# The opening of a one-core transformer step: rows for silu loaded first, weights of two groups behind them without waits, norm weights spread by a matmul, x issued behind silu

## What is computed

```
mod = silu(c) @ w_mod + b_mod                      # c_ctx for the context tokens
shift1, scale1, gate1, shift2, scale2, gate2 = split(mod, 6)
h   = layer_norm_plain(x) * (1 + scale1) + shift1
z   = h @ w_in                                      # q, k, v, xr, gr
q, k = rms_norm(q, q_norm_g), rms_norm(k, k_norm_g) # then rotary on latent tokens
mix = concat(attention(q, k, v), rg_lru(xr, gr)) @ w_out
x   = layer_norm(ALPHA * x + gate1 * mix)
x   = layer_norm(ALPHA * x + gate2 * expert_choice_ffn(h2))   # 16 experts
```

## Time and profile before

| | us |
|---|---|
| median of 3 runs | 945.56 (943.97 to 945.8) |
| profiled execution | 944.97 |
| its span | 943.2 |
| TensorE (PE) busy in the span | 882.9 |
| VectorE (DVE) busy | 774.0 |
| ScalarE (ACT) busy | 576.1 |
| GpSimd (POOL) busy | 160.8 |
| first matmul of group 0 | 12.88 |
| first transpose of x | 39.02 |

### The profile page before, as it was taken

One profiled execution on the slowest core, in us unless ns is written; L12 is line 12 of the kernel. 1 busy time (PEld: TensorE's weight loads), 2 busy tenths in 40 slices (PEclk: granted clock), 3 DMA queues, 4 the chain that ended last, 5 costly groups with the idle time before them and its releaser, 6 DMA issues.

```text
span 943.2 us, 11657 instructions
## 1 busy us (share of the span) xinstructions
PE 882.9 (94%) x4643; PEld 602.8 (64%) x4643; DVE 774.0 (82%) x802; ACT 576.1 (61%) x588; POOL 160.8 (17%) x108
## 2 busy tenths in 40 slices
PE   2899999889999976999999999999999999999995
PEld 0389978356678843666666666666666666666663
DVE  2777736578779887888989989998998998998877
ACT  1344367735751343777777777777777777677653
POOL 1000300010011014203203303303302311320220
PEclk9899999999999986999999999999999999999999
DMA  8930500663048387999999999999999999999716
GB/s 281 396 129 1 207 1 1 262 162 114 1 152 314 138 322 286 362 419 386 415 393 385 417 389 392 410 396 391 401 403 387 390 409 382 384 414 388 275 15 200
DMA packets 57358, 272.81 MB, mean 289 GB/s; under 512 B 6788, under 2 KB 7032, under 8 KB 40920
## 3 DMA queue, kind: packets, MB, share of 16 engines
q1 hardware_dynamic: 48264, 242.76, 65.7%
q0 software_dynamic: 7600, 24.06, 9.2%
q10 hardware_dynamic: 1440, 5.24, 1.4%
HBM read 258.05 MB, written 14.00 MB: 288 GB/s over the span
## 4 chain that ended last, share of the span: by engine, by line
PE 85%; DMA 5%; DVE 5%; ACT 2%; issue 1%; SPq 1%; ACTq 0%; DVEq 0%
PE PS L918 24%; PE PS L920 24%; PE PS L919 24%; DMA ring<-in_w_mod 4%; PE PS L932 2%; PE PS L1081 2%; PE PS L1065 2%; PE PS L1035 1%; PE PS L1104 1%; PE PS L1223 1%; PE PS L1236 1%; DMA acc_scratch<-ysc,idx_u 1%; PE PS L1159 1%; DVE smin L1558 1%; ACT prob L721 1%
## 5 line engine op out<-in xcount | busy, mean ns | idle before, releaser
L1737 DVE TENSOR_TENSOR Wl<-wr,Wh 128x2048 fp32r<-128x2048 f32 x190 | 432.4, 2289 | 50.1 <-ACT Wh L832 50.1
L832 ACT ACTIVATE Wh<-wr 128x2048 fp32r<-128x2048 f32 x192 | 367.3, 1915 | 67.6 <-PE PS L920 67.6
L918 PE MATMUL PS<-Wh,Xh 128*80 128x512 f32 x512 | 202.4, 395 | 1.5 <-DVE Xl L1742 0.8
L920 PE MATMUL PS<-Wl,Xh 128*80 128x512 f32 x512 | 201.0, 393 | 0.0
L919 PE MATMUL PS<-Wh,Xl 128*80 128x512 f32 x512 | 200.8, 392 | 0.0
L543 POOL DMA_INDIRECT acc_scratch<-ysc,idx_u x15 | 81.2, 5410 | 418.6 <-DVE ysc L1768 418.6
L920 PEld LDWEIGHTS PS<-Wl,Xh 128*80 128x80 f32 x512 | 75.7, 148 | 42.1
L918 PEld LDWEIGHTS PS<-Wh,Xh 128*80 128x80 f32 x512 | 75.7, 148 | 41.8 <-issue 1.2
L918 PE MATMUL PS<-Wh,HTh 128*80 128x512 f32 x256 | 101.6, 397 | 0.0
L919 PEld LDWEIGHTS PS<-Wh,Xl 128*80 128x80 f32 x512 | 75.8, 148 | 39.4
L919 PE MATMUL PS<-Wh,HTl 128*80 128x512 f32 x256 | 100.4, 392 | 0.0
(11 more groups left out here) (298 smaller groups left out, 1211.4 us busy)
## 6 DMA issues: line engine op xcount, KB each, us to landing
wr<-in_w_gate_up SPq DMA_DIRECT2D x128, 1024.0 KB, 13.6
wr<-in_w_down SPq DMA_DIRECT2D x64, 1024.0 KB, 12.3
ring<-in_w_mod SPq DMA_DIRECT2D x24, 1024.0 KB, 9.0
xt<-in_x_sample ACTq DMA_DIRECT2D x8, 512.0 KB, 8.6
ring<-in_w_in SPq DMA_DIRECT2D x4, 1024.0 KB, 12.4
ring<-in_w_out SPq DMA_DIRECT2D x4, 1024.0 KB, 11.9
w_qkv<-in_w_in SPq DMA_DIRECT2D x4, 768.0 KB, 10.2
h_scratch<-h POOLq DMA_DIRECT2D x5, 512.0 KB, 5.8
```

What stands on the lines that cost most here:

```text
L832: act.activation(Wh[n % NWH][:], wr[s][:], ACT.Copy).then_inc(W_hi, 1)
L918: pe.matmul(out, w[0], x[0], start=first, stop=False)
L920: return pe.matmul(out, w[0], x[1], start=False, stop=last)
L1737: dve.tensor_tensor(Wl[s][:], wr[s][:], Wh[n % NWH][:].bitcast(F32), ALU.subtract).then_inc(W_lo, 1)
```

## The change

The parts:

1. SyncE issues only `c` and the constants, then units 0 to 3 into `ring`, units 4 to 7 into a place of their own (`w_mod1`, where `Hh` and `Hl` lie later), `w_qkv` and the router's weights, all without a wait. The rows have a tile of their own, `rows`.
2. ScalarE issues `c_ctx`, `b_mod` and the two norm weights (each one row of 64) first, then the six other rows on another counter, `more_in`. It loads silu's table, computes silu, and only then issues x.
3. TensorE transposes the first 64 rows, and multiplies a column of ones with the row of the norm weights, which spreads it over 128 partitions. The other rows are transposed after group 0.
4. VectorE computes `gtab` at once. The decay rates stand between the statistics of chunk 2 and chunk 3.
5. GpSimd issues the cache's transfers behind its power.
6. The counters `x_again` are gone, `x_in` is used a second time for the same chunks.

```diff
     @block.sync
     def _(sp):
-        for r0, src in ((R_C, ...), (R_CTX, ...), (R_BM, ...), ...):
-            sp.dma_start(ring[r0:r0 + src.shape[0], 7, 0:P], src).then_inc(rows_in, 16)
-            if r0 == R_C:
-                sp.dma_start(consts[:], t["consts"][:, 0:P + 256]).then_inc(rows_in, 16)
+        sp.dma_start(rows[R_C:R_CTX, :], t["c"][0].rearrange("(r p) -> r p", p=P)).then_inc(rows_in, 16)
+        sp.dma_start(consts[:], t["consts"][:, 0:P + 256]).then_inc(rows_in, 16)
...
-        for u in range(8):
-            stream(u, slots(u), w_mod_v[:, 2 * (u % 4):2 * (u % 4) + 2, u // 4, :])
+        for u in range(4):
+            stream(u, slots(u), w_mod_v[:, 2 * u:2 * u + 2, 0, :])
+        for m in range(4):
+            sp.dma_start(w_mod1[:, 2 * m:2 * m + 2, :], w_mod_v[:, 2 * m:2 * m + 2, 1, :]).then_inc(mod1_in[m], 16)
...
     @block.gpsimd
-        pool.dma_start(gqk[:, 0, :], t["q_norm_g"][0].partition_broadcast(P)).then_inc(cache_in, 16)
-        pool.dma_start(gqk[:, 1, :], t["k_norm_g"][0].partition_broadcast(P)).then_inc(cache_in, 16)
...
     @block.scalar
     def _(act):
-        act.wait_ge(rows_in, 16 * 10)
+        act.dma_start(rows[R_CTX:R_BM, :], t["c_ctx"].rearrange("(r p) -> r p", p=P)).then_inc(rows_in, 16)
+        act.dma_start(rows[R_BM:R_CW, :], t["b_mod"][0].rearrange("(r p) -> r p", p=P)).then_inc(rows_in, 16)
+        act.dma_start(grow[:, 0:HD], t["q_norm_g"]).then_inc(rows_in, 16)
+        act.dma_start(grow[:, HD:P], t["k_norm_g"]).then_inc(rows_in, 16)
+        for r0, src in (...):
+            act.dma_start(rows[r0:r0 + src.shape[0], :], src).then_inc(more_in, 16)
+        act.wait_ge(ct_zero, 2)
+        act.activation(table_scr[:, 1:2], epsc[:], ACT.Silu)
+        act.wait_ge(cols_ok, 1)
+        act.activation(cT[:, :, 0], cols[:, R_C:R_C + 8], ACT.Silu).then_inc(ct_ok, 1)
+        act.activation(cT[:, :, 32], cols[:, R_CTX:R_CTX + 8], ACT.Silu).then_inc(ct_ok, 1)
         for c in range(CH):
             src = x_s[:, c, :] if c < PC else t["x_prompt"][0]
             act.dma_start(xt[:, c, :], src).then_inc(x_in[c], 16)
...
     @block.tensor
-        pe.wait_ge(rows_in, 16 * 10)
-        pe.transpose(bank(7, 0, R_END), ring[0:R_END, 7, 0:P], ident[0:R_END, 0:R_END]).then_inc(rows_t, 1)
+        pe.wait_ge(rows_in, 16 * 6)
+        pe.wait_ge(ct_zero, 2)
+        pe.transpose(bank(7, 0, R_CW), rows[0:R_CW, :], ident[0:R_CW, 0:R_CW]).then_inc(rows_t, 1)
+        pe.matmul(bank(7, 256, 256 + P), ones[:], grow[:], start=True, stop=True).then_inc(rows_t, 1)
...
         mod_group(0, 0)
-        mod_group(1, 4, range(0, 4))
+        pe.wait_ge(more_in, 16 * 6)
+        pe.transpose(bank(7, P, P + R_END), rows[0:R_END, :], ident[0:R_END, 0:R_END]).then_inc(rows_t, 1)
+        mod_group(1, None, range(0, 4))
...
     @block.vector
         for c in range(CH):
+            if c == 3:
+                decay_rates()
             dve.wait_ge(x_in[c], 16)
             last = layer_stats(xt[:, c, :], c)
         last.then_inc(var_ok, 1)
```

More of the change, by code:

```diff
@@ L222, in _build @@
     Z = Fz + 19456
+    rows, grow, ones = at("rows", [P, P], Fz + 2048), at("grow", [1, P], Fz + 2560), at("ones", [1, P], Fz + 3072)
     m_rowA = [at("m_rowA0", [P, H2], Fz), at("m_rowA1", [P, H2], Fz + 4096)]
@@ L450, in _ @@
         link(pool.memset(mhalf[:], -0.5))
+        pool.memset(ones[:], 1.0).then_inc(ct_zero, 1)
+        pool.wait_ge(var_ok, 1)
+        pow_mhalf(rstd[:], mv[:, :, 1], CH, 1.0).then_inc(rstd_ok, 1)
         for h in range(2):
@@ L928, in mod_group @@
             for k in ks:
-                if k % 2 == 0:
+                if k % 2 == 0 and g == 1:
+                    pe.wait_ge(mod1_in[k // 2], 16)
+                elif k % 2 == 0:
                     landed_wait(pe, u0 + k // 2)
+                src = w_mod1 if g == 1 else ring
                 for half in range(2):
                     last = pe.matmul(PS[MG * half:MG * half + MG, 512 * b:512 * b + 512], cT[:, k, :],
-                                     ring[:, k, 512 * half:512 * half + 512], start=(k == 0), stop=(k == KC - 1))
+                                     src[:, k, 512 * half:512 * half + 512], start=(k == 0), stop=(k == KC - 1))
                 last.then_inc(mod_used, 1)
@@ new lines, in _, with decay_rates @@
+        for g in range(2):
+            for w in range(2):
+                for c in range(PC):
+                    dve.tensor_tensor(gtab[:, g, w, c, :].rearrange("p (a b n) -> p a b n", a=2, b=2),
+                                      gqk[:, g, :].rearrange("p (a b n) -> p a b n", a=2, b=2),
+                                      rope[:, c, w, :].rearrange("p (a n) -> p a n", a=2).unsqueeze(2).broadcast_to([P, 2, 2, 16]),
+                                      ALU.mult)
+        def decay_rates():
+            dve.wait_ge(rows_t, 3)
+            link(dve.tensor_copy(cols[:, R_CW:R_END], bank(7, P + R_CW, P + R_END)))
+            link(dve.tensor_scalar(lscr[:, 1, :], cols[:, R_LAM:R_LAM + 8], -1.0, None, ALU.mult))
+            dve.tensor_tensor(lscr[:, 0, :], lscr[:, 1, :], cols[:, R_LAM:R_LAM + 8], ALU.max).then_inc(cols_ok, 1)
+            dve.wait_ge(lam_e, 1)
+            u, s, z, acc = nsp[:, 2, :], lscr[:, 2, :], lscr[:, 3, :], nsp[:, 1, :]
+            link(dve.tensor_scalar(s, u, 2.0, None, ALU.add))
+            link(dve.reciprocal(z, s))
+            link(dve.tensor_tensor(s, u, z, ALU.mult))
+            link(dve.tensor_tensor(z, s, s, ALU.mult))
+            link(dve.tensor_scalar(acc, z, 1.0 / 19.0, None, ALU.mult))
+            for m in (17, 15, 13, 11, 9, 7, 5, 3):
+                link(dve.scalar_tensor_tensor(acc, acc, 1.0 / m, z, ALU.add, ALU.mult))
+            link(dve.scalar_tensor_tensor(acc, acc, 1.0, s, ALU.add, ALU.mult))
+            link(dve.tensor_scalar(z, lscr[:, 1, :], 0.0, C_LRU, ALU.max, ALU.mult))
+            link(dve.scalar_tensor_tensor(acc, acc, 2.0 * C_LRU, z, ALU.mult, ALU.add))
+            dve.tensor_scalar(nsp[:, 0, :], acc, -1.0, None, ALU.mult).then_inc(nsp_ok, 1)
```

89 lines of the change are left out of this document (28 added, 61 removed).

## The result

| | before | changed |
|---|---|---|
| median, us | 944.86 (943.97 to 945.8, 7 runs) | 940.11 (937.76 to 941.83, 7 runs) |
| profiled execution, its span | 944.97, 943.2 | 941.66, 939.8 |
| w_mod's first piece issued / first packet | 4.51 / 7.70 | 1.60 / 2.90 |
| last unit of group 1 used | 37.16 | 32.33 |
| x scaled | 34.51 | 34.58 |

The ratio of the times is 0.9948 (95% interval 0.9932 to 0.9963): the change saves 4.75 us by the medians, and 3.5 to 6.4 by the interval. The forecast was 940.8, a gain of 4.8 from the 945.56 that three runs had given; the median of seven is 944.86. Times of packets and of a transfer's completions come from the trace's single records and count from the start of the span, as the rows do.

The account below looks back on a forecast made before the run. PE bounds the kernel after an opening that is one full, late-starting w_mod transfer. The last unit 4.9 us earlier, less a tenth for the second path, gave 4.8: from the 945.56 median to 940.8 us, range 938.6 to 943.5.

Parts of the forecast that it names:

- Start of the weights: Opening: w_mod issued at 1.60, 2.0 us lag; 4.4 plus half of 1.0 brings group 1's last unit 4.9 us earlier.
- Rival C: Opening: weights still flow 3.5 us after issue, and slowly; gain only 2.9 us, 942.7; chance 0.10.
- Waits of units 4 to 7: w_mod's stream: dropping these units' waits costs and gains nothing, since the 409 GB/s rate hides them.
- Rows and silu: Opening on ScalarE: rows land near 4.3, silu ends near 6.2, x is issued at 6.2; doesn't set the end.
- second path: Opening: x, statistics, decay rates and scaling, beside w_mod's path; forecast to end 0.7 us before it.
- Statistics and decay rates: VectorE in the opening: free at 23.9 to 25.7, statistics end 27.5 to 28.7, xn ready at 33.4.
- Rival B: Opening: the statistics' path sets the end, group 0 late by 1.7 and 2; gain about 3, 942.5; chance 0.12.
- Table, caches: Norm weights' table (2.25 us on VectorE, moved to about 6 us) and caches issued near 30: off the path, nothing.
- Nothing later gives it back: Behind the first x transpose, PE, ScalarE and VectorE feed one another, so the 4.8 us gain stays.
- rival F: Behind 39 us: the gain is made and lost again in a clock stretch or a gap; 945.6; chance 0.04.
- Rival E: Opening DMA: x served behind the queued weights, landing near 38, first transpose at 45; 952 us; chance 0.04.
- Rival D: TensorE's clock: a 6.8 us low stretch on the last units loses 3.0 us; gain 1.8, 943.8; chance 0.06.

Follow-up runs that it names:

- e2: Changed kernel with the ten small transfers issued by SyncE ahead of w_mod instead of by ScalarE; 945.55 us, ratio 1.0013.
- e7: Kernel before, with only the norm weights' two broadcasts replaced by two rows on ScalarE's queue and a matmul that spreads them; 941.45 us, ratio 0.9974.
- e8: e2 with the decay rates' copy moved behind chunk 4's statistics and their series behind the q/k/v steps; 942.74 us, ratio 0.9986.
- e9: e5 with c's rows and the constants moved from SyncE's queue to the front of ScalarE's, so w_mod is issued first; 941.03 us, ratio 0.9975.
- e5: Changed kernel with VectorE's decay series moved from ahead of chunk 3's statistics to behind the q/k/v steps; 938.71 us, ratio 0.9945.
- e5_again: e5 run a second time, on one chip with the unchanged changed kernel; 938.03 us, ratio 0.9945.
- e10: Changed kernel with VectorE's sixteen operations for `gtab` put back behind the scaling of x; 941.15 us, ratio 0.9964.
- e1: Changed kernel with GpSimd again issuing the two 32 KB norm-weight broadcasts, into a spare tile nobody reads; 943.03 us, ratio 0.9989.
- e3: Changed kernel with units 4 to 7 back in `ring`, each issued behind `mod_used`; 939.73 us, ratio 0.995.
- c1: Control: the changed kernel run again, unchanged; 939.46 us, ratio 0.9944.
- c2: The changed kernel once more, unchanged, on one chip with e5_again and e9; 938.73 us, ratio 0.9946.
- e4: Changed kernel plus two plain 32 KB transfers from GpSimd at the start, with rows that differ, into a spare tile; 939.27 us, ratio 0.995.

## Why the prediction was right, and where it was off

**Start of the weights: right, and in part by luck.** Expected 4.9 us at the last unit, measured 37.16 - 32.33 = 4.83. The first packet moved by 4.80: 2.91 by the issue, 1.9 by the lag from issue to packet, 3.2 before and 1.3 now. I had put the lag at 2.0; without broadcasts ahead of it, it is 1.0 to 1.3 (e2, e7, e8 and e9 at the lower end). From the first packet to the last completion the stream took 29.4 us before and takes 29.4 now. Where no fetch falls into it, it takes 28.6 to 28.8 (e2, e5, e5_again, e10; e8 and e9 have other small transfers beside it and take 29.4 and 30.0). So the half microsecond that I had added was there, and a little more, and the delay of the last completion took it back; I had neither the shorter lag nor this delay in the sum, and the two nearly cancel. Rival C didn't come: its 3.5 us of lag would have stayed. That the lag was the broadcasts' is shown by e7 alone. In e1 w_mod is issued ahead of them and the lag stays at 1.4; there they slow the stream that is already under way.

**Waits of units 4 to 7: right**, nothing (e3).

**Rows and silu: mis-sized, and the second path pays for it.** The step "land, by state_h's 2.3 us, near 4.3" failed: they landed at 6.83 (5.34 to 6.83 in the nine profiles with this order), beside the stream of weights; ahead of it, in e2 and e8, the same row took 1.3 and 2.0 us. Silu ended at 8.85 instead of 6.2 and x was issued at 8.54. That chunk 0 was used at 15.43, at the old time, hides the loss. From x's issue to chunk 0's use it was 9.1 us before, and it is 6.9 to 7.2 in the nine profiles with the weights ahead and no broadcasts (after, c1, c2, e3, e4, e5, e5_again, e9, e10). Issued at 6.2, chunk 0 would have been used near 13.2 and chunk 2 done near 20.0, ahead of `rows_t` 3: an estimate from these numbers, which no run tested by itself. e9 shows the price of three more microseconds.

**Statistics and decay rates: the term that was mis-sized.** "Xn is ready at 32.9 to 34.1, I say 33.4"; it was 34.58, and 34.14 in c1_after. "DVE is free at 23.9 to 25.7" was reckoned from when PE raises `rows_t` 3, and that was in time (20.3). What I left out stands in front on the same engine: chunk 2's statistics, which by the spacing of the chunks in the earlier trace rows begin at 20.8 and end at 22.3 (measured 20.70 and 22.23). The series then ends at 26.4 and the last chunk's statistics at 29.25 instead of 27.5 to 28.7. So the second path ended last by 0.37 us where it was to have 0.7 to spare, and the first transpose moved by 4.39 us, not 4.8. Rival B's mechanism is real (e2: 6.5 us); its point, group 0 late by two microseconds, was not reached.

**Table, caches: right** that they aren't on the path of the changed kernel; what the table's old place costs, e10 leaves open. But 16 instructions on VectorE are also 16 places in its program, and that moved a fetch (e10).

**"Nothing later gives it back": right** on the whole, by the table of experiments, and only within the scatter. Against the profile before, VectorE's operations in the profile after stand 4.4 us ahead at 200 us and 3.3 behind 220. In c1_after they go from 4.9 to 5.9 ahead there and lose 2.3 between 330 and 400, and c2_after ends 5.9 ahead. The low stretch of PE's clock at 176.6 to 180.0 in the profile after is not there in c1_after, and runs of one kernel spread over 4 us (937.76 to 941.83). That is rival F as noise, and that the medians differ by 4.75 us where the first transpose moved by 4.39 and 4.8 was forecast is as close as it is by luck.

Rival E did not come. Rival D did not set an end: a low stretch of 6.8 us lay at 23.6 to 30.4 in e3, where one unit took 3.68 us and one 2.87, and the first transpose was at 34.32 all the same. In e9 one lay on the last two units (30.1 to 33.6; 5.35 us for the two), hidden behind VectorE. D's sum was too high: at 3.68 us a unit, 1.8 units and not 2.7 fit into 6.8 us, so 2.1 us and not 3.0.

## What to carry to other kernels

When an opening is one full transfer, look for the stretch in which the DMA is busy and moves little, and ask which transfer reads the same row again and again; spreading the row on the chip costs matmuls of 0.79 us and a copy of 0.29. Before calling a second path free, write down everything that stands ahead on its engine, not only the signal that it waits for: here a margin of 0.7 us was a deficit of 0.4. And an order that puts a wait for the first path inside the second turns 2.5 us of delay into 6.5.

## What was not expected of the hardware

- Two broadcasts of 32 KB from one row of HBM hold 33.7 us of DMA engine time beside the stream (e1), two plain transfers of the same size 2.9 (e4).
- A row of 256 bytes issued beside a starting stream of weights lands 3.3 to 4.8 us after its issue (2.05 to 6.83 in the profile after), 7.1 with the stream ahead of it (e9, 3.07 to 10.18), and 1.3 and 2.0 without one (e2, 2.66 to 3.92, and e8).
- One instruction fetch of 8 KB, 0.34 us on one of the sixteen engines, coincides with a last completion 0.35 to 0.98 us behind the others in seven profiles, and the delay is gone in the six in which the fetch comes after the unit. In six of the seven it is longer than the fetch itself, up to three times; why isn't settled. In the kernel before the fetch delays no last completion.
